# Latent attention: two heads weighed side by side on the column halves, the division moved into the turning, and each tile turned one period later

## The reference, cut to what matters

```python
q = to_heads(rms_norm(c_q, mla_q_a_norm[l]) @ mla_w_uq[l], MLA_HEADS)      # 8 heads, 96 wide
kv = to_heads(rms_norm(c_kv, mla_kv_a_norm[l]) @ mla_w_ukv[l], MLA_HEADS)
k_nope, v = kv[..., :MLA_NOPE], kv[..., MLA_NOPE:]                         # v is 64 wide
...
def causal_block_attention(q, k, v):        # over blocks of 128 queries
        sc = jnp.einsum('bhqd,bhkd->bhqk', qi, kf) * scale
        sc = jnp.where(key_idx[None, :] <= q_idx[:, None], sc, -jnp.inf)
        p = jax.nn.softmax(sc, axis=-1)
        return jnp.einsum('bhqk,bhkd->bhqd', p, vf)
...
h = h + jnp.concatenate([o_gla, o_mla], axis=-1) @ w_out[l]
```

## Time and profile before

| | us |
|---|---|
| three runs: median (lowest to highest) | 3289.29 (3280.35 to 3292.79) |
| the profiled execution | 3288.64 |
| its span (first to last instruction) | 3286.9 |
| TensorE busy in the span | 3084.5 (94%) |
| VectorE, ScalarE, GpSimd busy | 1876.9, 953.0, 805.7 |
| first scores of the second latent tile to the first output product of the fourth part | 340.44 to 604.63 |

### The profile page before, as it was taken

How to read it: one execution, slowest core, us unless ns; L and a number is a source line. 1 busy time by engine, 2 the same in 40 slices (tenths; PEclk the granted TensorE clock), 3 DMA queues, 4 the chain that set the end, 5 groups by cost and what they waited for, 6 DMA issues and landing times. The chain is left out here.

```text
span 3286.9 us, 38717 instructions
## 1 busy us (share of the span) xinstructions
PE 3084.5 (94%) x15406; PEld 2442.3 (74%) x15406; DVE 1876.9 (57%) x2775; ACT 953.0 (29%) x1838; POOL 805.7 (25%) x478
## 2 busy tenths in 40 slices
PE   8999888888999999999899999998998999999888
PEld 6777777667788888888677777776676777777666
DVE  4334565543654154254578888888444267777773
ACT  3232444324211000001324333334212244444431
POOL 3221000151433233333223323232132221121101
PEclk9998999989999999999999999999999999999999
DMA  3012000010211111112211112122331110000021
GB/s 123 33 33 94 13 1 14 14 64 26 70 45 51 45 45 51 51 45 70 75 47 46 71 45 71 46 71 78 128 102 65 45 33 27 27 26 32 8 78 64
DMA packets 47739, 170.27 MB, mean 52 GB/s; under 512 B 5200, under 2 KB 5472, under 8 KB 46688
## 3 DMA queue, kind: packets, MB, share of 16 engines
q1 hardware_dynamic: 45856, 161.85, 14.5%
q0 software_dynamic: 1728, 6.29, 0.6%
HBM read 145.06 MB, written 23.07 MB: 51 GB/s over the span
## 5 line engine op out<-in xcount | busy, mean ns | idle before, releaser
L193 PE MATMUL acc<-x_hi,w_hi 128*128 128x512 f32 x2048 | 843.6, 412 | 46.8 <-POOL w_lo L188 23.4
L186 POOL CAST w_hi<-w_raw 128x1024 fp32r<-128x1024 f32 x217 | 236.7, 1091 | 2408.6 <-PE acc L195 1434.8
L194 PE MATMUL acc<-x_lo,w_hi 128*128 128x512 f32 x2048 | 820.6, 401 | 0.0
L195 PE MATMUL acc<-x_hi,w_lo 128*128 128x512 f32 x2048 | 819.9, 400 | 0.0
L188 POOL TENSOR_TENSOR w_lo<-w_raw,w_hi 128x1024 fp32r<-128x1024 f32 x217 | 544.8, 2510 | 17.3
L193 PEld LDWEIGHTS acc<-x_hi,w_hi 128*128 128x128 f32 x2048 | 391.8, 191 | 152.9 <-issue 38.8
L195 PEld LDWEIGHTS acc<-x_hi,w_lo 128*128 128x128 f32 x2048 | 391.6, 191 | 95.5
L194 PEld LDWEIGHTS acc<-x_lo,w_hi 128*128 128x128 f32 x2048 | 392.4, 192 | 90.2 <-issue 2.4
L2509 DVE SCALAR_TENSOR_TENSOR acc<-ev_upad,cols,acc 128x1024 f32<-128x1024 f32 x232 | 298.2, 1285 | 5.0
L193 PE MATMUL aux<-x_hi,w_hi 128*128 128x512 f32 x464 | 198.8, 428 | 2.2 <-POOL w_lo L188 2.2
L195 PE MATMUL aux<-x_hi,w_lo 128*128 128x512 f32 x464 | 184.3, 397 | 0.0
(11 more groups left out here) (506 smaller groups left out, 5029.4 us busy)
## 6 DMA issues: line engine op xcount, KB each, us to landing
w_raw<-in_stream SPq DMA_DIRECT2D x217, 512.0 KB, 3.4
h<-in_x SPq DMA_DIRECT2D x16, 512.0 KB, 9.8
spill_h<-h SPq DMA_DIRECT2D x8, 512.0 KB, 5.2
spill<-ev_zst SPq DMA_DIRECT2D x8, 512.0 KB, 3.0
h_even<-spill_h SPq DMA_DIRECT2D x8, 512.0 KB, 7.8
ev_zr<-spill SPq DMA_DIRECT2D x8, 512.0 KB, 3.6
spill_h<-h_even SPq DMA_DIRECT2D x8, 512.0 KB, 5.4
h<-spill_h SPq DMA_DIRECT2D x8, 512.0 KB, 4.6
```

What stands on the lines that cost most here:

```text
L186: pool.tensor_copy(k.w_hi[slot][:], k.w_raw[slot][:]).then_inc(k.w_split, 1)
L193: pe.matmul(out, w_hi, x_hi, start=start, stop=False)
L194: pe.matmul(out, w_hi, x_lo, start=False, stop=False)
L195: return pe.matmul(out, w_lo, x_hi, start=False, stop=stop)
```

## The change

**Turning.** `turn` is no longer a transposition with the identity but a product with a diagonal matrix `diag`, which holds the inverse of each row's sum. VectorE makes it for each tile (`weights`: a reciprocal of the tile's sums, then identity times that column), so `output` goes.

**One period later.** The turning of tile `t` and its copies are issued in the period of tile `t + 1` (`hm, tm` is the tile before the period's), in a flat loop of 65 periods. The projections move from periods 0 and 1 to 2 and 3.

**Weighing.** Even heads are turned and copied into `kept`, which holds all 36 blocks of a head. In the odd heads `weigh` takes both heads: values are now the weights (128x64), the turned blocks move (128 columns), the even head writes PSUM partitions 0 to 63 and the odd one 64 to 127. What comes out is already turned, 128 columns for each tile, in one bank for tiles 0 to 3, 5 and 7 and another, shared with the projections, for tiles 4 and 6.

**The end.** `turn_o` goes. `high` and `low` run for each tile of a pair, in the periods of the odd head and shortly after, and `weigh` of a tile waits until the low part of the tile before it in its bank is taken.

```diff
-    o_tok = k.at("mla_o", 80, [P, TT, H * MLA_V])
+    kept = k.at("mla_kept", 80, [P, TT * (TT + 1) // 2, P])
+    diag = k.at("mla_diag", 119, [P, 2, P])
...
+    def turned_out(t):
+        bank = 2 if t in (4, 6) else 3
+        return aux[:, bank * HALF:bank * HALF + P]
...
-                pe.wait_ge(s["exped"], TT * h + t + 1)
+                pe.wait_ge(s["diag"], TT * h + t + 1)
                 for j, kb in enumerate(g):
-                    mm = pe.transpose(bank(key)[:, j * P:(j + 1) * P], pr[:, t % 2, kb * P:(kb + 1) * P], k.ident)
+                    mm = pe.matmul(bank(key)[:, j * P:(j + 1) * P], pr[:, t % 2, kb * P:(kb + 1) * P], diag[:, t % 2, :], start=True, stop=True)
...
             def weigh(h, i):
+
                 t, g = GROUPS[i]
+                n = TT * (h // 2) + t
+                wait_used(pe, ("p", h - 1, i))
                 wait_used(pe, ("p", h, i))
                 if i == 0:
                     pe.wait_ge(s["vt_done"], h + 1)
-                    pe.wait_ge(s["o_read"], h + 1)
+                if t == 4 and g[0] == 0:
+                    pe.wait_ge(s["z_copied"], 4 * min(h + 3, H))
+                if g[0] == 0 and n:
+                    pe.wait_ge(s["m_lo"], n if t < 4 else n - 1)
+                out = turned_out(t)
                 for j, kb in enumerate(g):
-                    mm = pe.matmul(aux[:, 3 * HALF + t * MLA_V:3 * HALF + (t + 1) * MLA_V], pT[:, i % 2, j * P:(j + 1) * P],
-                                   vt[h % 2][:, kb, :], start=kb == 0, stop=kb == t)
+                    pe.matmul(out[0:MLA_V, :], values_of(h - 1)[:, kb, :], kept[:, kept_at(t, kb), :], start=kb == 0, stop=kb == t)
+                    mm = pe.matmul(out[MLA_V:P, :], values_of(h)[:, kb, :], pT[:, i % 2, j * P:(j + 1) * P], start=kb == 0, stop=kb == t)
...
+            def period(n):
+
+                (h, t), (hm, tm) = divmod(n, TT), divmod(n - 1, TT)
+                more, ahead, i = h + 1 < H, h + 2 < H and t in (2, 3), FIRST_GROUP[tm]
+                if n + 1 < TT * H:
+                    scores(*divmod(n + 1, TT))
+                if ahead:
+                    project(h + 2, 2 * t - 4)
+                if n:
+                    turn(hm, i)
+                    if hm % 2 and i:
+                        weigh(hm, i - 1)
+                    if hm and hm % 2 == 0 and i == 0:
+                        weigh(hm - 1, NG - 1)
+                if ahead:
+                    project(h + 2, 2 * t - 3)
                 if more and t in (5, 6):
                     turn_qk("qk"[t - 5], h + 1, 0)
...
+                if n and tm >= 4:
+                    turn(hm, i + 1)
+                    if hm % 2:
+                        weigh(hm, i)
                 if more and t in (5, 6):
                     turn_qk("qk"[t - 5], h + 1, 1)
...
+            def weights(h, t):
+                n = TT * h + t
+                dve.wait_ge(s["exped"], n + 1)
...
+                dve.reciprocal(st[:, 27, t % 2:t % 2 + 1], sums_of(h)[:, t:t + 1]).then_inc(s["inverse"], 1)
+                dve.wait_ge(s["inverse"], n + 1)
+                dve.tensor_scalar(diag[:, t % 2, :], k.ident, st[:, 27, t % 2:t % 2 + 1], None, ALU.mult).then_inc(s["diag"], 1)
...
+            def period(n):
+                (h, t), (hm, tm) = divmod(n, TT), divmod(n - 1, TT)
+                if n + 1 < TT * H:
+                    tile_max(*divmod(n + 1, TT))
+                if n < TT * H:
+                    weights(h, t)
+                if n and tm >= 4:
+                    copy_turned(dve, hm, FIRST_GROUP[tm])
+                if n >= 3 and (n - 3) // TT % 2:
+                    low(read_at(n - 3))
+                if h + 1 < H and t < 6:
+                    PREPARE[t](h + 1)
```

More of the change, by code:

```diff
@@ L968, in ring_order @@
                 yield (which, 0, c), ACTE
[L969 to L976, removed]
+        for n in range(TT * H + 1):
+            (h, t), (hm, tm) = divmod(n, TT), divmod(n - 1, TT)
+            if n:
+                yield ("p", hm, FIRST_GROUP[tm]), DVEE if tm >= 4 else ACTE
+            for c in range(2):
+                if t in (5, 6) and h + 1 < H:
+                    yield ("qk"[t - 5], h + 1, c), ACTE
+                if n and tm >= 4 and c == 0:
+                    yield ("p", hm, FIRST_GROUP[tm] + 1), ACTE
     USE, freed, counts = {}, [], {ACTE: 0, DVEE: 0}
@@ L1097, in project @@
                     pe.wait_ge(s["z_copied"], h * 4 + tp)
+                if h >= 4 and h % 2 == 0 and tp == 0:
+                    pe.wait_ge(s["m_lo"], TT * (h // 2 - 1) - 1)
                 for u in range(2):
@@ L1114, in turn_qk @@
                 mm.then_inc(s["ring_full"], 1)
[L1116 to L1124, removed]
             pe.wait_ge(s["squares"], 3)
@@ L1151, in _ @@
             scores(0, 0)
[L1153 to L1164, removed]
+            def period(n):
[5 more added lines that the diff above has]
+                    project(h + 2, 2 * t - 4)
+                if n:
+                    turn(hm, i)
[5 more added lines that the diff above has]
+                    project(h + 2, 2 * t - 3)
                 if more and t in (5, 6):
                     turn_qk("qk"[t - 5], h + 1, 0)
[L1167 to L1172, removed]
+                if n and tm >= 4:
+                    turn(hm, i + 1)
+                    if hm % 2:
+                        weigh(hm, i)
                 if more and t in (5, 6):
                     turn_qk("qk"[t - 5], h + 1, 1)
-            for h in range(H):
-                for t in range(TT):
-                    period(h, t)
+            for n in range(TT * H + 1):
+                period(n)
             weigh(H - 1, NG - 1)
-            turn_o(2)
             def m_ready(q):
-                if q == 3:
-                    turn_o(3)
-                pe.wait_ge(s["m_lo"], q + 1)
+                pe.wait_ge(s["m_lo"], TT * (q + 1))
             for i in range(KD):
-                if i == 1:
-                    pe.wait_ge(s["o_read"], H + 1)
                 wout(1, i, slots[i % 2], m_ready if i == 0 else None)
@@ L1255, in _ @@
             exponent(0, 0)
-            def period(h, t):
-                nxt, more, ahead = following(h, t), h + 1 < H, h + 2 < H
-                i = FIRST_GROUP[t]
+            def period(n):
+                (h, t), (hm, tm) = divmod(n, TT), divmod(n - 1, TT)
+                more, ahead, i = h + 1 < H, h + 2 < H and t in (2, 3), FIRST_GROUP[tm]
                 if more and t == 0:
                     estimate(h + 2, st[:, 16:18, :], st[:, 18:20, :])
[L1262 to L1269, removed]
+                if ahead:
+                    copy_projected(h + 2, 2 * t - 4)
+                if n and tm < 4:
+                    copy_turned(act, hm, i)
+                if ahead:
+                    copy_projected(h + 2, 2 * t - 3)
                 if more and t in (5, 6):
                     copy_qk("qk"[t - 5], h + 1, 0)
[L1272 to L1276, removed]
+                if n + 1 < TT * H:
+                    exponent(*divmod(n + 1, TT))
+                if n and tm >= 4:
+                    copy_turned(act, hm, i + 1)
                 if more and t in (5, 6):
                     copy_qk("qk"[t - 5], h + 1, 1)
-                if not more and t < 7:
+                if n >= 2 and (n - 2) // TT % 2:
+                    high(read_at(n - 2))
+                if h == H - 1 and t < 7:
                     if t == 0:
@@ L1284, in period @@
                         mem_norm.square(act, 7)
[L1286 to L1290, removed]
+            for n in range(TT * H + 1):
+                period(n)
+            high(TT * H // 2 - 1)
             mem_norm.root_of(act)
@@ L1441, in period @@
                     (q_squares, k_squares)[t - 6](h + 2)
[L1442 to L1445, removed]
+                if h == H - 1 and t >= 2:
                     mem_norm.sum(dve, t - 1)
-                if not nxt:
+                if n == TT * H - 1:
                     mem_norm.sum(dve, t)
[L1450 to L1455, removed]
+            for n in range(TT * H + 1):
+                period(n)
+            low(TT * H // 2 - 2)
+            low(TT * H // 2 - 1)
             for i in range(KD):
```

62 lines of the change are left out of this document (37 added, 25 removed).

## The result

| | before | after |
|---|---|---|
| median of six runs, us (lowest to highest) | 3286.64 (3280.35 to 3292.79) | 3298.27 (3297.55 to 3299.09) |
| ratio of the times, with its 95% interval | | 1.0043 [1.0032, 1.0054] |
| the profiled execution, and its span | 3288.64, 3286.9 | 3299.09, 3297.3 |
| the stage, first scores to the first output product of part four | 264.19 | 276.99 |
| the rest of the span | 3022.7 | 3020.3 |

The change makes the kernel 0.4% slower, 11.6 us by the medians. The kernel before was run again beside the experiments, 23 and 30 times, with medians of 3282.40 and 3282.05 us; against those the changed kernel, which was not run again, would be some 16 us slower. So the cost in whole times is uncertain by some 4 us. All of it is in the stage, which grew by 12.8 us in the profiled executions.

The account below looks back on a forecast made before the run. TensorE was taken to set the pace of the latent-head stage, idle a little in each head. Terms +31.1 - 12.2 - 3.6 - 4 + 3.6 + 1 - 3 = +12.9 us gave 3302 us, range 3279 to 3321.

Parts of the forecast that it names:

- the likeliest case: Whole kernel: the forecast itself holds, 3294 to 3308 us, chance 0.42.
- Turning, +31.1: TensorE, 288 blocks: a float32 product takes 0.22 us where a transposition takes 0.112, so 0.108 us more each.
- Weighing, -12.2: TensorE: 144 pairs at 0.215 us plus 48 visits at 0.36 make 48.3 us, against 60.5 before.
- the halves don't pair: Rival, weighing: column halves don't run side by side, 31 us more, 3333 us in all; chance 0.03.
- The turn of the outputs and the end, -3.6 and -4: Stage's end: 32 transpositions go, -3.6 us; the chain of divide, turn, high and low part goes, -4 us.
- VectorE: Each tile: a new reciprocal and diagonal take 0.45 us, standing ahead of the copy TensorE waits for.
- The waits in the steady pair: TensorE, even and odd head: waits of 10.6 us a pair, 5.3 a head against 4.7; +3.6 us for six heads.
- Head 0, -3: First head: starts with nothing to turn or weigh and loses its first tiles' small waits, -3 us.
- The clock: Stage: low clock cost 5.9 us before, and an equal cost was assumed after.
- The rival of more low clock: From even tile 5 to odd tile 1: two or three dear stretches add 12 to 18 us, 3314 to 3320; chance 0.25.
- The lag hides the waits: Rival, stage: copies come early enough that the waits go, about 36 us less, 3266 us; chance 0.07.
- No low clock at all: Rival, stage: turnings as real products fill TensorE more; without the 5.9 us it is 3296; chance 0.10.

Follow-up runs that it names:

- the first experiment: Kernel before, with the turning as a float32 product with the identity instead of a transposition: 3297.67 us, ratio 1.0051 to the kernel before.
- the third experiment: Changed kernel, with each group's products issued for the even head first, then the odd head: 3309.15 us, ratio 1.0084 to the kernel before.
- The fourth: Changed kernel, with tile 2's output in the bank of tiles 4 and 6: ratio 1.0013 to the kernel before, stage 266.52 us.
- fifth: Changed kernel, with VectorE's two diagonal operations behind the period's copy and low part: ratio 1.0025 to the kernel before, stage 269.47 us.
- sixth experiments: Changed kernel, with ScalarE's last copies of period 6, including the next head's keys, ahead of tile 7's exponent: ratio 1.0029 to the kernel before.
- the second experiment: Changed kernel, with the turning a transposition again and the division by the sums left out: ratio 1.0026 to the kernel before.
- three edits of a few lines: Changed kernel, with tile 2 in the other bank, diagonal behind the copy, and keys' copy ahead of the exponent: ratio 0.9978 to the kernel before.

## Why the prediction was right, point by point

The forecast was 3302 us, the measurement 3298.27, inside the likeliest case (3294 to 3308) and within 0.5% of before. The rise was to be 12.9 us and is 11.6 by the six runs. The stage was to take 277 us and took 276.99. That is closer than the terms deserve: part of it is luck.

- **Turning, +31.1.** Right in size: 0.112 us a block by the first experiment, forecast 0.108.
- **Weighing, -12.2.** Inside a visit as forecast, 0.215 a pair. The edges cost 0.30 us and not 0.36, so, if all 48 visits were like those read, 48 x 0.06 = 2.9 us more are saved: -15.1. The rival that the halves don't pair is out by the same rows, and the third experiment shows what less pairing costs.
- **The turn of the outputs and the end, -3.6 and -4.** The turn is gone, and so is the listed wait of 3.3 us for the last low part. The first product of part four (618.02) has no wait. The last tile's parts were hidden, as said.
- **VectorE.** Reciprocal and diagonal take 0.41 us from start to start, forecast 0.45.
- **The waits in the steady pair.** Each came where it was put. In us, forecast and then measured in heads 3 and 4: odd tile 1 0.7, 0.30; low part of tile 1 1.2, 1.05; of tile 2 1.9, 1.72; odd period 6 0.85, 0.63; new even head 0.9, 0.77; projection 0.35, 0.19; even tile 5 1.3, 1.00; tile 6 1.4, 1.13; keys 2.0, 1.76. Together 10.6 and 8.55. The brackets leave out the tail of a record, about 0.16 each; with nine of them it is 10.0. The fourth, fifth and sixth experiments removed or shortened them one kind at a time, and the time followed.
- **Head 0, -3.** From its first maximum to head 1's, 29.93 us before and 26.97 after. The agreement proves little, since turning and weighing also moved in it.
- **What missed.** Turning, weighing and outputs as measured (+32, -15, -3.6) come to +13.6. The waits, the start and the end then make +1.4 where I had -2.4: 3.8 us more. Of that the pace of the steady pairs holds little (70.4 against 70 us); the rest is in the first and last heads. From head to head, at full clock, the change costs -3.0 us in head 0, +14.7 in heads 1 to 5, and +3.3 in heads 6 and 7 with the end (70.91 us with 1.2 of low clock, where it was 72.29 with 5.9). Which term of the first and last heads was too hopeful, no run separates.
- **The clock.** I assumed equal cost and it was 2.2 us cheaper. At an equal clock the change costs 15.0 us, not 12.9. Two errors of 2 us cancel. The rival of more low clock did not come, though its place was right: the stretches begin at the boundary behind even heads, in three of the four, but last 3.4 us each and not as long as the old one of 17.1. I had priced each like the old one.
- **The lag hides the waits.** It does not, as argued: each wait is for work of the same period. The rival's premise, that VectorE has time to spare, is true (175.71 us busy of 276.99, 63%) and does not help.

No low clock at all was a rival at 0.10. The first experiment bears on it: with turnings as products the stage before had none, and with transpositions it had 17.1 us. With transpositions in the kernel after there were 27 us for 10. The Trainium skill, TensorE: Matmul & The Clock Gate, Part 4, says that transpositions don't count as busy as products do, and these four traces agree in direction. But the kernels with transpositions also waited more (33.5 and 53.9 us against 17.0 and 37.8), and two with products and fewer waits than the change, those of the fourth and the fifth experiment, had more low clock than it (13.6 us each for 10.2). Each figure is also that of one execution, and that of the first experiment had the highest mean clock of its six (0.978, the others 0.974 to 0.976), while that of the kernel before ranges from 0.972 to 0.977 in its 53 later runs. So the cause of the low clock stays open.

## What to carry over

Where an engine sets the pace but stands idle 13% of the time, as TensorE in this stage, an idle stretch can be the end of a chain on another engine that starts with one of its own results. Add up that chain link by link, and count each new instruction that is put ahead of the link the busy engine waits for: it can cost its full length at every such wait, while work taken from the busy engine inside one gives little (25.9 us of TensorE's busy time for 9.2 in the second experiment). Before a faster form is given up, look at which bank its sums share and what stands ahead of a copy: here three edits of a few lines, which removed no instruction, were worth 21 us, more than the change had lost.

## What the runs showed of the hardware that was not expected

- By the recorded starts, products on two column halves need not start in program order: a record of the second half started at 392.49, ahead of one of the first half at 392.59 that stands before it. Pairs issued one half after the other still overlap in part (1.51 us a visit for 1.03 by turns).
- Entering and leaving the half-width form costs about 0.30 us. The Trainium skill, TensorEngine Tiling (Array Packing), Key Properties, says that a change of the tiling mode drains the engine. A price at the edges fits that, though the trace shows no drain as such; here it is a third of the 0.86 us that four pairs take.
- The low clock came in stretches of 3.4 us, 6.8 and 17.1, with the same kernel code around them at one head and not at the next: behind the wait of 1.76 us for the keys it came at heads 2, 4 and 6 and not at head 0.
